# RWKV units of a two-layer backbone step: the next unit's decay work and matrix products in other places of the level order

## What is computed

```
def rwkv_scan(r, w, k, v, a, b, s0):
    def step(s, inp):
        rt, wt, kt, vt, at, bt = inp
        sa = jnp.einsum('bhij,bhj->bhi', s, at)
        s = s * wt[..., None, :] + sa[..., :, None] * bt[..., None, :] + vt[..., :, None] * kt[..., None, :]
        return s, jnp.einsum('bhij,bhj->bhi', s, rt)
```

## Time and profile before

| | us |
|---|---|
| median of 3 runs | 3899.51 (3883.81 to 3903.02) |
| the profiled execution | 3888.84 |
| its span, first to last instruction | 3887.0 |
| ten RWKV units, about 1015 to 1515 us of the span | 500 |

### The profile page before, as it was taken

One profiled execution on the slowest core, in us unless ns is written; L12 is line 12 of the kernel. 1 busy time (PEld: TensorE's weight loads), 2 busy tenths in 40 slices (PEclk: granted clock), 3 DMA queues, 4 the chain that ended last, 5 costly groups with the idle time before them and its releaser, 6 DMA issues.

```text
span 3887.0 us, 52585 instructions
## 1 busy us (share of the span) xinstructions
PE 3428.2 (88%) x21383; PEld 3045.3 (78%) x21383; DVE 1267.6 (33%) x1862; ACT 996.1 (26%) x1361; POOL 336.1 (9%) x366
## 2 busy tenths in 40 slices
PE   8799998969577877899999979999897689899998
PEld 1399998959466665899998169999897656899998
DVE  0222222245455554322221032222314435322222
ACT  0232122222321122332120033122224435332121
POOL 0000001000444441100000000000101000100001
PEclk9899999969788887999999989999997879999999
DMA  8522121101000000122222822122110100122121
GB/s 312 174 76 77 60 86 55 34 31 50 3 4 1 1 1 22 60 76 76 65 81 78 303 90 82 64 70 81 44 49 12 33 3 27 58 73 76 65 88 42
DMA packets 79087, 260.64 MB, mean 67 GB/s; under 512 B 20112, under 2 KB 20240, under 8 KB 78704
## 3 DMA queue, kind: packets, MB, share of 16 engines
q1 hardware_dynamic: 77568, 250.79, 19.4%
q0 software_dynamic: 1392, 8.07, 0.5%
HBM read 255.02 MB, written 3.81 MB: 67 GB/s over the span
## 4 chain that ended last, share of the span: by engine, by line
PE 82%; DVE 7%; ACT 4%; POOL 3%; issue 3%; DMA 1%; DVEq 0%; SPq 0%; ACTq 0%; POOLq 0%
PE ps L1988 30%; PE ps L1989 30%; PE ps L2009 6%; PE ps L893 1%; PE ps L1817 1%; DVE normed L2266 1%; DVE h_lo L2253 1%; PE ps L884 1%; PE ps L1797 1%; DMA ring<-w_ada 1%; PE ps L1500 1%; POOL h_mem L2357 1%; PE ps L1805 1%; PE ps L873 1%; PE ps L837 1%
## 5 line engine op out<-in xcount | busy, mean ns | idle before, releaser
L315 DVE TENSOR_TENSOR w_lo<-ring,w_hi 128x1024 fp32r<-128x1024 f32 (+1 forms) x305 | 399.0, 1309 | 1867.7 <-ACT w_hi L310 1867.7
L310 ACT ACTIVATE w_hi<-ring 128x1024 fp32r<-128x1024 f32 (+1 forms) x305 | 343.0, 1126 | 1522.0 <-PE ps L1989 1501.8
L1988 PE MATMUL ps<-h_hi,w_hi 128*128 128x320 f32 x1928 | 609.7, 316 | 126.0 <-DVE h_lo L2253 58.5
L1989 PE MATMUL ps<-h_hi,w_hi 128*128 128x320 f32 x1928 | 602.3, 312 | 0.0
L1988 PE MATMUL ps<-h_lo,w_hi 128*128 128x320 f32 x1928 | 601.9, 312 | 0.0
L1989 PE MATMUL ps<-h_lo,w_hi 128*128 128x320 f32 x1928 | 601.8, 312 | 0.0
L1988 PE MATMUL ps<-h_hi,w_lo 128*128 128x320 f32 x1928 | 601.6, 312 | 0.0
L1989 PE MATMUL ps<-h_hi,w_lo 128*128 128x320 f32 x1928 | 601.5, 312 | 0.0
L1988 PEld LDWEIGHTS ps<-h_hi,w_hi 128*128 128x128 f32 x1928 | 367.2, 190 | 145.2 <-issue 80.7
L1989 PEld LDWEIGHTS ps<-h_hi,w_hi 128*128 128x128 f32 x1928 | 368.4, 191 | 0.0
L1988 PEld LDWEIGHTS ps<-h_lo,w_hi 128*128 128x128 f32 x1928 | 367.9, 191 | 0.0
(11 more groups left out here) (348 smaller groups left out, 4527.0 us busy)
## 6 DMA issues: line engine op xcount, KB each, us to landing
ring<-w_ada SPq DMA_DIRECT2D x144, 512.0 KB, 4.5
ring<-w_up0a SPq DMA_DIRECT2D x44, 512.0 KB, 3.4
ring<-w_up0b SPq DMA_DIRECT2D x44, 512.0 KB, 3.3
ring<-w_up1a SPq DMA_DIRECT2D x44, 512.0 KB, 3.3
ring<-w_up1b SPq DMA_DIRECT2D x44, 512.0 KB, 3.3
ring<-w_down0a SPq DMA_DIRECT2D x16, 704.0 KB, 4.0
ring<-w_down0b SPq DMA_DIRECT2D x16, 704.0 KB, 4.0
ring<-w_down1a SPq DMA_DIRECT2D x16, 704.0 KB, 4.1
```

The lines of the kernel that those rows point to most:

```text
L310: act.activation(w_hi[:, n % SPLITS, 0:cols], ring[:, r, 0:cols], ACT.Copy).then_inc(high_ready, 1)
L315: dve.tensor_tensor(w_lo[:, n % SPLITS, 0:cols], ring[:, r, 0:cols], w_hi[:, n % SPLITS, 0:cols].bitcast(F32), ALU.subtract).then_inc(spli ...
L1988: pe.matmul(left, weights, acts[:, k, LEFT], start=start, stop=stop)
L1989: mm = pe.matmul(right, weights, acts[:, k, RIGHT], start=start, stop=stop)
```

## The change

Nothing is added or taken out; instructions change places in the five loops, and two waits take another count. In the diff `...` marks what is left out.

```diff
 # POOL
                     if n >= 2:
-                        pool.wait_ge(rw_y, 4 * n - 5)
+                        pool.wait_ge(rw_y, 4 * n - 6)
...
                 if core:
                     merging(u, 4)
+                    merging(u, 5)
                 if ahead:
                     decayed(u + 1, 0)
-                if core:
-                    merging(u, 5)
-                if ahead:
                     decayed(u + 1, 1)
 # TensorE
+                if ahead and u >= 0:
+                    low_w(u + 1)
                 if core:
                     turned(u, 1)
                     widened(u, 1)
                 if ahead and u >= 0:
-                    low_w(u + 1)
+                    low_a(u + 1)
                 if core:
                     merged(u, 1)
-                if ahead and u >= 0:
-                    low_a(u + 1)
-                if core:
                     turned(u, 2)
...
                     widened(u, 4)
-                if behind:
-                    state(u - 1, 0)
+                if ahead:
+                    matrices(u + 1, 0)
                 if core:
                     merged(u, 4)
                 if behind:
-                    state(u - 1, 1)
+                    state(u - 1, 0)
                 if core:
                     turned(u, 5)
                     widened(u, 5)
                 if ahead:
-                    matrices(u + 1, 0)
+                    matrices(u + 1, 1)
                 if core:
                     merged(u, 5)
-                if ahead:
-                    matrices(u + 1, 1)
+                if behind:
+                    state(u - 1, 1)
...
                 if ahead:
                     matrices(u + 1, 2)
-                    both_turned(u + 1)
                 if core:
                     merged(u, 6)
                 if ahead:
+                    both_turned(u + 1)
+                    natural(u + 1, 0)
                     matrices(u + 1, 3)
-                    natural(u + 1, 0)
                     natural(u + 1, 1)
 # ScalarE: tanh_w ahead of widened 1, tanh_a ahead of widened 2, right_side ahead of
 # widened 3, exponentials ahead of widened 4, spread_state behind widened 6
...
 # VectorE: raw_w ahead of turned 1, log_decay and raw_a ahead of step 1; running in two parts
+                if ahead and u >= 0:
+                    running(u + 1, 0)
+                if core:
                     step(u, 2)
                 if ahead and u >= 0:
-                    last = running(u + 1)
+                    turn(running(u + 1, 1))
+                    centred(u + 1)
                 if core:
                     step(u, 3)
-                if ahead and u >= 0:
-                    turn(last)
-                    centred(u + 1)
...
                 if core:
                     step(u, 4)
+                if ahead:
+                    masked(u + 1, 0)
                 if behind:
                     new_state(u - 1, 0)
-                    new_state(u - 1, 1)
-                if ahead and u >= 1:
-                    first_state(u + 1)
-                if ahead:
-                    masked(u + 1, 0)
...
                 if ahead:
                     masked(u + 1, 1)
+                if behind:
+                    new_state(u - 1, 1)
                 if core:
                     grown(u, 6)
                 if ahead:
                     first_merge(u + 1)
                     other_half(u + 1, 1)
+                if ahead and u >= 1:
+                    first_state(u + 1)
+                if ahead:
                     masked(u + 1, 2)
                     masked(u + 1, 3)
 # VectorE, waits: add_outputs and new_state
-                dve.wait_ge(rw_y, 4 * n + 2 * d + 1)
+                dve.wait_ge(rw_y, 4 * n + d + 1)
...
-                dve.wait_ge(rw_y, 4 * n + 2 * d + 2)
+                dve.wait_ge(rw_y, 4 * n + d + 3)
```

More of the change, by code:

```diff
@@ L1140, in scalar_rwkv @@
                 core, ahead, behind = 0 <= u < RW_N, u + 1 < RW_N, u >= 1
-                if core:
-                    widened(u, 1)
                 if ahead and u >= 0:
@@ L1145, in scalar_rwkv @@
                 if core:
-                    widened(u, 2)
+                    widened(u, 1)
                 if ahead:
                     tanh_a(u + 1)
+                if core:
+                    widened(u, 2)
                 if behind:
@@ L1151, in scalar_rwkv @@
                 if core:
+                    right_side(u)
                     widened(u, 3)
-                    right_side(u)
-                    widened(u, 4)
                 if ahead:
@@ L1157, in scalar_rwkv @@
                 if core:
+                    widened(u, 4)
                     widened(u, 5)
+                    widened(u, 6)
                 if ahead and u >= 1:
                     spread_state(u + 1)
-                if core:
-                    widened(u, 6)
                 if ahead:
@@ L1210, in log_decay, with running @@
                                        ALU.mult, ALU.add))
[L1212 to L1220, removed]
+            def running(n, d):
+                if d == 0:
+                    if n:
+                        dve.wait_ge(rw_prep, 2 * n)
+                    dve.memset(rw_dn[:, :, :, 0:1], 0.0)
+                for b in range(2):
+                    last = dve.tensor_tensor_scan(rw_dn[:, d, b, 1:P + 1], C("ones"), rw_w[:, d, b, :], 0.0,
+                                                  ALU.mult, ALU.add)
                 return last
@@ L1318, in vector_rwkv @@
             log_decay(0)
-            turn(running(0))
+            running(0, 0)
+            turn(running(0, 1))
             centred(0)
@@ L1336, in vector_rwkv @@
                 core, ahead, behind = 0 <= u < RW_N, u + 1 < RW_N, u >= 1
-                if core:
-                    turned(u, 1)
                 if ahead and u >= 0:
@@ L1341, in vector_rwkv @@
                 if core:
-                    step(u, 1)
+                    turned(u, 1)
                 if ahead and u >= 0:
@@ L1346, in vector_rwkv @@
                 if core:
+                    step(u, 1)
+                if ahead and u >= 0:
+                    running(u + 1, 0)
+                if core:
                     step(u, 2)
                 if ahead and u >= 0:
-                    last = running(u + 1)
+                    turn(running(u + 1, 1))
+                    centred(u + 1)
                 if core:
                     step(u, 3)
-                if ahead and u >= 0:
-                    turn(last)
-                    centred(u + 1)
                 if behind:
```

## The result

| | before | changed |
|---|---|---|
| median (us) | 3901.27 (3883.81 to 3904.11, 4 runs) | 3847.51 (3840.49 to 3853.24, 4 runs) |
| span of the profiled execution (us) | 3887.0 | 3845.2 |

The ratio is 0.9871, with an interval of 0.9837 to 0.9904: faster by some 54 us, where 3888 had been forecast and the range ended at 3852.

The account below looks back on a forecast made before the run. No single engine was taken as full: levels hang on each other, TensorE waits in order and its clock falls. Moves −3.3 us and middle falls −7.8 us made −11.1, giving 3888 us on the median; range 3852 to 3921.

Parts of the forecast that it names:

- a fall in every unit again, short and long mixed as now: TensorE's clock after the rest at each unit's end: still falls every unit, as that rest grows from 4.06 to 4.4 us.
- the moves: Reordered instructions at the upper clock, start to end of a unit: −0.37 us a unit, ends −1.5 and +0.7.
- falls in the middle: Wait before `widened` 5, where the clock fell three times, goes: 3 × 2.61 = −7.8 us.
- The rival of the early clock: After units' ends the clock comes back early each time; six long falls become short, −32 us, 3856 us; chance 0.34.
- Start: Start of a unit: both low-rank products ahead of `merged` 1, `natural` 0 moved away; +0.59 us a unit.
- Level 2 to 3: ScalarE copies `right_side` ahead of `widened` 3, so TensorE's wait before `outputs` 0 goes; −1.05 us a unit.
- Level 3 to 4: First product `matrices` 0 ahead of `merged` 4 makes TensorE wait about 1.9 us for GpSimd's `decayed`; +1.15 us a unit.
- the rival on the slow side: New wait before `matrices` 0 becomes a clock fall in each unit; 3921 us, chance 0.16.
- Level 4 to 5: `merging` 5 is done early, so the wait before `widened` 5 goes; 5.7 us instead of 6.98, −1.28 us a unit.
- Level 5 to 6: Same pattern as the level before, `new_state` fitting beside it on VectorE; 5.7 us instead of 6.79, −1.09 us a unit.
- End: End of a unit: `first_state` ahead of `masked` 2 delays the fourth product; +1.31 us, rest 4.06 to about 4.4 us.

Follow-up runs that it names:

- the two kernels with four products: Kernel before and changed kernel, each with four extra unused products of constants on TensorE in the rest ahead of the fourth product: 3846.34 and 3833.21 us.

## Why the prediction was wrong

The step that failed is "so I expect a fall in every unit again, short and long mixed as now". A fall in every unit was right. Their mix was not: long ones went from six to three and from 17 to 10.2 us. The price of a long one of 17 us over a short one is 5.40 us in the earlier trace rows. That of one of 10.2 us is in the `grown` 1 of three units in a row of the changed kernel, the first with a fall of 10.2 us, the second with a short one:

```profile
1201.77 0.69 DVE L1267 TENSOR_TENSOR h_mem<-h_mem,ps 128x512 f32<-128x512 f32 x1 [0.30 <-PE ps L891]
...
1249.11 0.69 DVE L1267 TENSOR_TENSOR h_mem<-h_mem,ps 128x512 f32<-128x512 f32 x1 [0.30 <-PE ps L891]
...
1293.73 0.69 DVE L1267 TENSOR_TENSOR h_mem<-h_mem,ps 128x512 f32<-128x512 f32 x1 [0.30 <-PE ps L891]
```

The units take 47.3 and 44.6 us, so it is 2.7 us, and the mix is worth 6 x 5.40 − 3 x 2.7 = 24 us. With 0.94 us a unit for the moves, 8.5 us, and 7.8 us for the falls in the middle it makes the 40 us by which the profiled executions differ over these nine units. The medians differ by 54: the profiled execution of the kernel before lay 12 us under its median, and no profile shows the falls of the others. The rival of the early clock was the nearest, but it left the moves too small and took the length of a long stretch as given: nothing behind the unit ends of the trace of before showed a stretch of 10 us, and the range had no place for it. The end of a unit was mis-sized with it: the rest that was to grow from 4.06 to 4.4 us shrank to 3.59.

Term by term, at the upper clock (start and end from the two kernels with four products):

- *Start*, forecast +0.59: +0.65. Confirmed as a loss. It also made level 1 to 2 0.20 us longer, which the sum did not have. The changed kernel with the start of before gains more than both, 20 us: there a unit with a short fall takes 42.5 us instead of 44.6, and none has a long one of 10.2 us behind its end.
- *Level 2 to 3*, −1.05: −1.29.
- *Level 3 to 4*, +1.15: +0.73. The wait ahead of `matrices` 0 is there, 1.45 us instead of 1.9, since `decayed` took 2.7 us (1171.48 to 1174.15) instead of 3.13. It did not become a fall in any unit, so the rival on the slow side did not come.
- *Level 4 to 5*, −1.28: −0.53. `other_half` took 1.59 us instead of 0.69 beside GpSimd's next mask, and `widened` 5 waited 0.92 us for it.
- *Level 5 to 6*, −1.09: −1.08.
- *End*, +1.31: +0.40. `first_state` takes 0.48 us in its new place instead of 1.39.
- *Falls in the middle*, −7.8: none is left, as forecast.

What the sum had −0.37 us for measured −0.94 a unit, inside its ends. What I did not draw from my own terms is that two of them, the start and the first product in level 4, are losses that could have been left out.

By the rule of the Trainium skill that I weighed ("TensorE: Matmul & The Clock Gate", Part 1: sustained activity releases the low clock) all stretches should have been short. The trace still does not agree: three of 10.2 us, TensorE busy 8.98 us of one.

## What to carry to other kernels

Where TensorE rests for some microseconds once in each turn of a loop, the granted clock behind the rest can be worth more than the waits one is moving: price both, and hold the clock up once with work of no use to see the moves alone. Time each part of a reordering by itself, since a part that its own levels show as a loss can hide under the clock's gain; here, leaving two parts out gained another 43 us. And compare medians of several runs, because such a kernel's executions can differ by 30 us with the same code.

## What the runs showed of the hardware

The length of a VectorE instruction hung on what GpSimd did beside it. In the changed kernel's timelines, VectorE and then GpSimd:

```profile
1177.25 1.59 DVE L1253 TENSOR_TENSOR h_mem<-h_mem,cst 128x512 f32<-128x512 f32 x1
...
1183.70 0.69 DVE L1253 TENSOR_TENSOR h_mem<-h_mem,cst 128x512 f32<-128x512 f32 x1
...
1191.35 0.48 DVE L1300 TENSOR_TENSOR h_mem<-h_mem,rest 128x128 f32<-128x128 f32 x2
```

```profile
1177.01 1.28 POOL L756 TENSOR_TENSOR cst<-rest,cst 128x512 f32<-128x512 f32 x1
```

`other_half` took 1.59 us where it began inside GpSimd's mask, which ran to 1178.29, and 0.69 us alone; `first_state` 0.48 us with GpSimd idle and 1.39 us beside its decay. The Trainium skill, "SBUF — State Buffer", "SBUF: two separate sides", says that a VectorE instruction with two SBUF inputs and a GpSimd instruction that reads SBUF take turns at a shared port, each for its whole length; these rows agree nearly: the mask's remaining 1.04 us and the 0.69 us alone would make 1.73, and 1.59 was measured.
